# A two-block transformer kernel: the residual and MLP norm through PSUM banks, another order of weights and single columns around the first output projection

## The reference

```python
# first block (gains and modulation vectors from c)
x = x + gt1 * rmsnorm(mix_x, g_post_mix)              # mix_x = mixed @ w_out
h2 = rmsnorm(x, g_pre_mlp) * (1 + sc2) + sh2
y_x = square(relu(h2 @ w_mlp_in)) @ w_mlp_out
x = x + gt2 * rmsnorm(y_x, g_post_mlp)
# second block, the part that needs no x
mem_h = rmsnorm(mem_2, norm_mem_2)                    # 256 tokens
k, v = split(mem_h @ w_mem_kv_2)                      # 512 features each
```

## Time and profile before

| | |
|---|---|
| median of 3 runs | 1445.64 us (1445.02 to 1448.01) |
| profiled execution | 1446.45 us |
| its span | 1445.2 us |
| mean granted TensorE clock | 0.982 |
| busy: PE, DVE, ACT, POOL | 95%, 42%, 38%, 49% |
| PE share of the chain that ended last | 72% (DVE 12%, POOL 7%, ACT 4%) |
| DMA, mean | 103 GB/s |

### The profile page before, as it was taken

The page is one execution under the profiler, slowest core; times in us unless marked ns, Lnnn a source line. Parts: engine busy times, 40 slices in busy tenths (PEclk is TensorE's granted clock), DMA queues, the critical chain, the costliest instruction groups (busy, mean ns, idle before and its releaser), DMA issues.

```text
span 1445.2 us, 16207 instructions
## 1 busy us (share of the span) xinstructions
PE 1367.7 (95%) x6458; PEld 1085.9 (75%) x6458; DVE 601.2 (42%) x836; ACT 546.8 (38%) x862; POOL 703.4 (49%) x375
## 2 busy tenths in 40 slices
PE   7999897979999999997998999999999999999999
PEld 4688676858888878885777777665677888888887
DVE  4795865564310052102727583855462211011110
ACT  4521764443432244323424535643343322223221
POOL 2534505833544434454468593543265654455542
PEclk9999998999999999998999999999999999999999
DMA  9564413513333323332222112111112323323332
GB/s 382 214 244 186 135 76 134 172 45 97 107 92 98 104 79 103 100 97 81 73 88 59 44 59 59 59 45 44 29 59 88 115 90 102 102 88 103 90 100 73
DMA packets 40650, 148.58 MB, mean 103 GB/s; under 512 B 4224, under 2 KB 4480, under 8 KB 39808
## 3 DMA queue, kind: packets, MB, share of 16 engines
q1 hardware_dynamic: 39696, 144.26, 30.4%
q0 software_dynamic: 448, 2.62, 0.5%
q10 hardware_dynamic: 432, 0.67, 0.1%
HBM read 144.65 MB, written 2.10 MB: 102 GB/s over the span
## 4 chain that ended last, share of the span: by engine, by line
PE 72%; DVE 12%; POOL 7%; issue 4%; ACT 4%; DMA 0%; DVEq 0%; POOLq 0%; ACTq 0%
PE bank L544 20%; PE bank L545 20%; PE bank L546 20%; POOL wL L2394 3%; POOL EE L2543 2%; PE bank L594 2%; PE bank L601 1%; DVE xT L1994 1%; PE bank L582 1%; PE bank L584 1%; PE bank L583 1%; POOL hL L2399 1%; DVE small L1929 1%; PE bank L896 1%; DVE acc L2099 1%
## 5 line engine op out<-in xcount | busy, mean ns | idle before, releaser
L2394 POOL TENSOR_TENSOR wL<-raw,wH 128x1024 fp32r<-128x1024 f32 (+1 forms) x205 | 501.3, 2447 | 495.3 <-ACT wH L1166 495.3
L544 PE MATMUL bank<-hH,wH 128*128 128x512 f32 x784 | 322.9, 412 | 33.5 <-POOL wL L2394 18.9
L545 PE MATMUL bank<-hL,wH 128*128 128x512 f32 x784 | 312.0, 398 | 0.0
L546 PE MATMUL bank<-hH,wL 128*128 128x512 f32 x784 | 311.4, 397 | 0.0
L1166 ACT ACTIVATE wH<-raw 128x1024 fp32r<-128x1024 f32 (+1 forms) x205 | 214.1, 1047 | 200.6 <-PE bank L546 163.1
L544 PEld LDWEIGHTS bank<-hH,wH 128*128 128x128 f32 x784 | 151.4, 193 | 78.8 <-issue 19.0
L546 PEld LDWEIGHTS bank<-hH,wL 128*128 128x128 f32 x784 | 151.0, 193 | 33.2
L545 PEld LDWEIGHTS bank<-hL,wH 128*128 128x128 f32 x784 | 151.4, 193 | 30.2 <-issue 1.7
L544 PE MATMUL bank<-gH,wH 128*128 128x512 f32 x352 | 138.4, 393 | 4.0 <-POOL wL L2394 4.0
L546 PE MATMUL bank<-gH,wL 128*128 128x512 f32 x352 | 137.7, 391 | 0.0
L545 PE MATMUL bank<-gL,wH 128*128 128x512 f32 x352 | 137.5, 391 | 0.0
(11 more groups left out here) (345 smaller groups left out, 2046.2 us busy)
## 6 DMA issues: line engine op xcount, KB each, us to landing
raw<-in_wall SPq DMA_DIRECT2D x205, 512.0 KB, 3.6
rows<-in_wall SPq DMA_DIRECT2D x24, 1024.0 KB, 10.1
bra<-in_rpbw SPq DMA_DIRECT2D x8, 360.0 KB, 4.5
xq<-in_xt SPq DMA_DIRECT2D x2, 1024.0 KB, 6.9
xT<-in_xn SPq DMA_DIRECT2D x1, 2048.0 KB, 7.9
out_x<-xT SPq DMA_DIRECT2D x8, 256.0 KB, 2.7
vE<-in_ctxt SPq DMA_DIRECT2D x1, 1024.0 KB, 19.7
icn<-in_invc POOLq DMA_DIRECT2D x1, 1024.0 KB, 8.7
```

The source lines that it names most:

```text
L544: matmul(o, a_h, b_h, start=first, stop=False)
L545: matmul(o, a_h, b_l, start=False, stop=False)
L546: return matmul(o, a_l, b_h, start=False, stop=last)
L2394: tt(wL[i % NHL][:, 0:n], raw[i % NRAW][:, 0:n], wH[i % NHL][:, 0:n].bitcast(F32), ALU.subtract).then_inc(s.w_lo, 1)
```

## The change

The edits, all between the value rows of `w_in` and the first tiles of `w_mlp_in`:

- **Post steps and MLP norm in PSUM.** The scaled `y` goes to bank 2 or 3 (in turn) and not back to `y`; its other factor, the root, stays in bank 7, where Ln and Exp now write. The addition to `xT` reads the bank. The same two banks take the place of two `tmp` tiles in the MLP norm, for the product with the root and the full value. All eight low parts `hL` are now VectorE's.
- **Sums in column groups.** ScalarE puts the squares of `xT` into `y`, whose tiles are free. Once four of them are there, four products with 32 columns of ones go into the four groups of 32 partitions of bank 6; a second four are added. VectorE copies the bank to `tmp` and one `statistic` sums the partitions into bank 7; each sum then comes 32 times over, and `root` divides by 32 x 1024. The eight full-width products are gone.
- **Order of `w_mem_kv_2`'s keys.** One tile after another; the list of weights follows. Two tiles share a bank. The statistic of `mix` comes after the first product of the second tile.
- **Single columns spread.** `late_column(sec, j)` is one product; section 2's stand between the value rows of `w_in`, sections 3 and 4 after each tile of `w_out` for k = 4 to 7, section 5's after each k of m=7. The statistic of `mem` moves to (3, 1). VectorE's `late_vector(3)` and `(4)` move behind `hm`.
- **Weights between the norms' tiles.** ScalarE and GpSimd make chunks within the loops over `hm`, the squares of `xT` and `h2`, one at a time.
- The banks of `w_mem_kv_2` and of the MLP follow another turn.

```diff
@@ -76,7 +76,8 @@
...
         tile("w_out", m, range(8))
-    group([("w_mem_kv_2", m) for m in range(4)], range(8))
+    for m in range(4):
+        tile("w_mem_kv_2", m, range(8))
...
@@ -316,26 +317,27 @@
 def _banks():
-    of, n = {}, 0
+    of, n, order = {}, 0, range(7)
...
         for t in tiles:
-            of[t] = n % 7
+            of[t] = order[n % 7]
...
     of.update((("w_out", m), b) for m, b in enumerate((6, 0, 4, 5, 1, 2, 3, 6)))
-    of.update((("w_mem_kv_2", m), b) for m, b in enumerate((0, 4, 5, 1)))
-    of.update((("mem_v", i), 2 + i) for i in range(2))
-    n = 4
+    of.update((("w_mem_kv_2", m), b) for m, b in enumerate((0, 0, 4, 4)))
+    of.update((("mem_v", i), b) for i, b in enumerate((5, 1)))
+    order, n = (4, 6, 0, 5, 1, 2, 3), 0
...
     turn(*(("w_in_2", m) for m in (10, 11, 12, 13, 6, 7, 8, 9)), *(("vt", i) for i in range(4)))
-    n = 0
+    order, n = range(7), 0
...
@@ -576,16 +580,16 @@
...
                 w_h, w_l, raise_ = weights(name, k, m0, 4)
-                for x, o in zip(tokens, outs):
+                for i, (x, o) in enumerate(zip(tokens, outs)):
...
                     mm = matmul(o, x_l, w_h, start=False, stop=n == len(ks) - 1)
-                if raise_:
-                    mm.then_inc(s.product, 1)
-                if beside is not None:
-                    beside(k)
+                    if raise_ and i == len(outs) - 1:
+                        mm.then_inc(s.product, 1)
+                    if beside is not None:
+                        beside(k, i)
@@ -640,15 +644,16 @@
             freed[7] = s.mod_ab, quarter + 1
-        def late_columns(*secs):
-            o = claim(7)
-            for i, sec in enumerate(secs):
-                pe.wait_ge(s.mod_acc, 8 * (sec - 1))
-                for j in range(8):
-                    mm = matmul(o[:, 8 * i + j:8 * i + j + 1], macc[sec % 2][:, 128 * j:128 * j + 128], ones[:, 0:1],
-                                start=True, stop=True)
+        def late_column(sec, j, at_=0):
+            if j == 0 and at_ == 0:
+                claim(7)
+            pe.wait_ge(s.mod_acc, 8 * (sec - 1))
+            mm = matmul(bank[7][:, at_ + j:at_ + j + 1], macc[sec % 2][:, 128 * j:128 * j + 128], ones[:, 0:1], start=True,
+                        stop=True)
+            if j == 7:
                 mm.then_inc(s.mod_sum, 1)
-            freed[7] = s.mod_late, secs[-1] - 1
+            freed[7] = s.mod_late, sec - 1
@@ -703,14 +708,15 @@
...
             freed[b3] = s.pool_y, g + 1
-        late_columns(2)
...
                     for i in range(n)]
-        def first_scores(k):
-            if k == 6:
+        def first_scores(k, i):
+            if 6 * k + i < 8:
+                late_column(2, 6 * k + i)
+            if (k, i) == (6, 5):
@@ -791,48 +797,63 @@
...
                 near_values(NEAR - 1)
-            if (k, m) == (2, 1):
-                late_columns(3, 4)
-            if (k, m) == (5, 3):
+            if (k, m) == (3, 1):
...
                 statistic("mem", [(acc[1][:, 0:256], 0, 128)], 256)
+            if k >= 4:
+                j = 4 * (k - 4) + m
+                late_column(3 + j // 8, j % 8, 8 * (j // 8))
...
         for m in range(4, 8):
-            tile("w_out", m, range(8), [(claim(BANK["w_out", m]), MX)])
+            tile("w_out", m, range(8), [(claim(BANK["w_out", m]), MX)],
+                 beside=(lambda k: late_column(5, k)) if m == 7 else None)
             freed[BANK["w_out", m]] = s.y_sq, m + 1
-            if m == 6:
-                late_columns(5)
...
             return hmH[:, k, :], hmL[:, k, :], s.rest_g if k % 2 else s.rest_v, REST.hm + k // 2 + 1
-        def mixer_statistic(k, m):
-            if (k, m) == (1, 3):
+        def mixer_statistic(k):
+            if k == 0:
...
                 statistic("mix", [(acc[0][:, :], 0, 128)])
-        kv = [("w_mem_kv_2", m) for m in range(4)]
-        group(kv, range(8), XM, mixer_statistic, 256)
+        for m in range(4):
+            o = claim(BANK["w_mem_kv_2", m])[:, 256 * (m % 2):256 * (m % 2) + 256]
+            tile("w_mem_kv_2", m, range(8), [(o, XM)], beside=mixer_statistic if m == 1 else None)
...
             freed[BANK["w_mem_kv_2", m]] = s.k_mem, m + 1
+        freed[7] = s.post, 16
         outs = [claim(BANK["mem_v", i]) for i in range(2)]
-        sums = claim(7)
-        def residual_sums(k):
-            pe.wait_ge(s.sq, SQ.xt + k + 1)
-            matmul(sums, ones[:, :], tm[2 + k % 2][:, :], start=k == 0, stop=k == 7).then_inc(s.xt_sum, 1)
+        def residual_sums(k, i):
+            if (k, i) in ((1, 1), (3, 1)):
+                half = k // 2
+                o = bank[6] if half else claim(6)
+                pe.wait_ge(s.sq, SQ.xt + 4 * half + 4)
+                for n in range(4):
+                    mm = matmul(o[32 * n:32 * n + 32, :], ones[:, 0:32], y[:, 4 * half + n, :], start=half == 0,
+                                stop=half == 1)
+                mm.then_inc(s.xt_sum, 1)
+            if (k, i) == (4, 1):
+                pe.wait_ge(s.add_v, ADD_V.xt + 1)
+                statistic("pre_mlp", [(tm[0][:, :], 0, 128)])
         rows("w_mem_kv_2", 4, range(8), tokens(hmH, hmL, XM, 2), outs, residual_sums)
-        freed[7] = s.root, logged("pre_mlp")
+        freed[6] = s.add_v, ADD_V.xt + 1
+        freed[7] = s.mult, MULT.h2 + 8
+        for b in (2, 3):
+            freed[b] = s.rest_v, REST.h2 + 8
...
         def X2(k):
-            return hH[:, k, :], hL[:, k, :], s.rest_g if k % 2 else s.rest_v, REST.h2 + k // 2 + 1
+            return hH[:, k, :], hL[:, k, :], s.rest_v, REST.h2 + k + 1
@@ -1176,12 +1197,9 @@
...
                 activation(dst, src, ACT.Copy, scale=scale).then_inc(sem, 1)
-        def root(name, features, dst, n=512, from_=None):
-            if from_ is None:
-                act.wait_ge(s.summed, summed(name))
-            else:
-                act.wait_ge(*from_)
+        def root(name, features, dst, n=512):
+            act.wait_ge(s.summed, summed(name))
@@ -1359,47 +1377,46 @@
...
             copy(hmH[:, j, :], tm[j % 2][:, 0:256], s.hi)
+            if j in (3, 7):
+                ahead("w_out", 7, 4 + j // 4, 1)
...
             mixer_tile(m)
-        for k in range(0, 8, 2):
-            ahead("w_mem_kv_2", k, 0)
-            if k == 2:
-                root("mix", 1024, rs[1])
+        ahead("w_mem_kv_2", 7, 0)
+        ahead("w_mem_kv_2", 7, 3, 1)
+        root("mix", 1024, STAT)
+        ahead("w_mem_kv_2", 0, 4, 1)
         for k in range(8):
-            ahead("w_mem_kv_2", k, 4)
             act.wait_ge(s.post, 2 * k + 2)
-            t = 2 + k % 2
-            room(t)
-            act.wait_ge(s.add_v, ADD_V.m + 7)
-            act.wait_ge(s.add_g, ADD_G.y + 7)
-            square(tm[t][:, :], xT[:, k, :], s.sq)
-            held[t] = s.xt_sum, k + 1
-            if k % 2:
-                m = k // 2
-                act.wait_ge(s.product, done("w_mem_kv_2", 7, m))
-                copy(kM[:, m, :], bank[BANK["w_mem_kv_2", m]][:, 0:256], s.k_mem)
-        act.wait_ge(s.full, FULL.hm + 8)
-        root("pre_mlp", 1024, rs[0], from_=(s.xt_sum, 8))
+            square(y[:, k, :], xT[:, k, :], s.sq)
+            if k in (0, 2, 5):
+                ahead("w_mem_kv_2", {0: 2, 2: 4, 5: 6}[k], 4, 1)
+        ahead("w_mlp_in", 0, 0, 1)
+        for m in range(4):
+            act.wait_ge(s.product, done("w_mem_kv_2", 7, m | 1))
+            copy(kM[:, m, :], bank[BANK["w_mem_kv_2", m]][:, 256 * (m % 2):256 * (m % 2) + 256], s.k_mem)
+        root("pre_mlp", 32 * 1024, STAT)
...
             act.wait_ge(s.mult, MULT.h2 + j + 1)
-            activation(hH[:, j, :], tm[j % 2][:, :], ACT.Identity, bias=mod[:, 24 + j, 0:1],
+            activation(hH[:, j, :], bank[2 + j % 2], ACT.Identity, bias=mod[:, 24 + j, 0:1],
                        scale=coef[:, 3, j:j + 1]).then_inc(s.hi, 1)
-        act.wait_ge(s.product, done("w_mem_kv_2", 7, 7))
-        for i in range(2):
-            copy(vM[:, i, :], bank[BANK["mem_v", i]], s.v_mem)
+            if j < 2:
+                act.wait_ge(s.product, done("w_mem_kv_2", 7, 7))
+                copy(vM[:, j, :], bank[BANK["mem_v", j]], s.v_mem)
+            if j in (1, 3):
+                ahead("w_mlp_in", j + 1, 0, 1)
...
             if m < 3:
-                act.wait_ge(s.rest_g, REST.h2 + 4)
-                act.wait_ge(s.rest_v, REST.h2 + 4)
-                act.wait_ge(s.xt_sum, 8)
+                act.wait_ge(s.rest_g, REST.hm + 4)
+                act.wait_ge(s.rest_v, REST.hm + 4)
+                act.wait_ge(s.add_g, ADD_G.y + 7)
...
@@ -1964,8 +1980,6 @@
...
             tt(acc[1][:, 0:256], acc[1][:, 0:256], tm[2 + j % 2][:, 0:256], ALU.add).then_inc(s.add_v, 1)
-        late_vector(3, 0, 4)
-        late_vector(4, 8)
@@ -1977,6 +1991,8 @@
...
                 rest(hmL[:, j - 1, :], tm[0][:, 0:256], hmH[:, j - 1, :], s.rest_v)
+        late_vector(3, 0, 4)
+        late_vector(4, 8)
@@ -1986,28 +2002,36 @@
...
```

(48 more changed lines are left out.)

4 lines of the change are left out of this document (2 added, 2 removed).

## The result

The changed kernel takes **1423.7 us** (median of 4 runs, 1423.4 to 1424.0), the kernel before 1445.3 beside it (4 runs, 1441.2 to 1448.0): a ratio of 0.985, with a 95% interval of 0.983 to 0.988. That is 21.6 us less, where 25.5 were forecast (1420.1, range 1411 to 1432). Its profiled execution took 1423.9 us, span 1422.5.

A forecast was written before the change was run, and what follows sets the result against it. TensorE, 95% busy, was taken as the bound: its work, waits and half-clock stretches. Gains of 7.3, 11.0, 8.6 and 0 sum to 26.9, less 1.4 is 25.5 us: 1421.0 profiled, 1420.1 us median, range 1411 to 1432 (own range 1414 to 1426).

The forecast's parts named there:

- Part 2: From the first w_mem_kv_2 product to the first w_mlp_in product: 26.5 us instead of 37.5, 11.0 us less.
- Part 3: From w_mlp_in's first product up to 340 us: 105 products in 23.8 us instead of 32.4, 8.6 us less.
- Part 1: Up to the first w_mem_kv_2 product, 270.1 us before: it ends at 262.8, 7.3 us earlier.
- The wait of 2.9 for chunk 6: In w_out: chunk 6's low part ready at 248.6, wanted by TensorE at 245.7, a wait of 2.9 us.
- 255.6, wanted at 254.1, another 1.5: In w_out: chunk 7's low part, its raw load queued behind rows loads, comes at 255.6; TensorE waits 1.5 us.
- the 1.4 us taken off at the end: Deducted from the 26.9 us sum for a half clock after the 2.9 us wait and for margins of 0.2 and 0.4.
- Rival D: Spread single columns lower TensorE's clock wherever they stand: +37 against -26 us, 1457 us; chance 0.04.
- sign of being wrong: Shift under 3 us at the first w_mem_kv_2 product, value rows waiting for squares, or clock falling beside spread columns.
- Part 4: Elsewhere: section 2's columns between the value rows, and the banks' new turn: 0 us, the latter bounded by -1 and +2.
- Rivals A: Part 1 gains nothing, as late rows, POOL's additions and SP's queue are hardly touched: 1426 to 1430 us; chance 0.16.
- B: The two forecast waits of part 1 vanish: 1411 to 1414 us; chance 0.09.
- C: The 32-column products run one after another (1425 us), or steps with a bank stand for POOL (1434); chance 0.06.

The follow-up runs named there:

- experiment one: The changed kernel with only VectorE's 16 post steps back in SBUF instead of the PSUM banks; 1439.3 us.
- e2_full_sums: Also cited as "two": the changed kernel with the eight 32-column products of the squares made 128 columns wide, one after another into bank 6; 1430.6 us.
- Experiment seven: The changed kernel without the two single w_mlp_in weight chunks inside the loop over h2; they are made after all eight hH; 1438.2 us.
- e6_block34: The changed kernel with sections 3 and 4's 16 columns in one block at (2,1), late_vector(3) and (4) ahead of hm; 1421.5 us.
- b1_all: The changed kernel with section 2's block, sections 3 and 4 spread earlier, section 5 in key tiles, mem statistic (3,2), last w_out raw load earlier; 1419.2 us.
- experiment three: The changed kernel with section 2's eight single columns back in one block ahead of w_in's value rows; 1424.8 us.
- b2_nosp: b1_all with the changed kernel's SP queue order, the last w_out raw load again behind rows pair 23; 1420.9 us.

## Why the prediction was right, and where it was off

**Part 2 was right, step by step.** Pairs of post steps in 1.39 us (forecast 1.5; 272.58 to 283.7 is 11.1, forecast 12.1), none over 0.76; experiment one shows the mechanism, two the price of the sums. 27.2 us against 26.5: TensorE waits 0.4 for h2's first low part (forecast 0.2), and the rest is its own work, 26.9 us where I had 26.2.

**Part 3 was right.** 105 records in 23.8 us where 23.8 was forecast. The affine step from bank to bank was 0.81 and not 0.74; VectorE's margin covers it. Experiment seven shows what the two chunks inside the loop hold off: 14.7 us. What VectorE's making the odd low parts is worth by itself was not run.

**Part 1 had the right change, and a wrong chain of small waits.** 5.4 us instead of 7.3.
- The mem statistic waited 1.5 (forecast 1.6); moved, it is worth 7.7 us. hm took 11.9 us (222.9 to 234.8) against a forecast of 12 to 13 from 220.8. Right.
- The wait of 2.9 for chunk 6 did not come. I gave GpSimd's three additions their 6.74 us of the earlier trace rows; they took 5.22, since VectorE still stood for the last spread column when the first of them ran. Chunk 6 was ready 8.2 us after the late rows began, not 13.3. Where the late rows begin earlier (`e6_block34`, `b1_all`), the three take 6.7 and 6.8 us and a wait for chunk 6 comes, 1.8 and 1.9 us.
- A wait of 0.7 at 223.6, for the first chunk after the statistic, was not in the sum: ScalarE makes two wH only from 220.0 on, behind the squares of xm, and the first of GpSimd's two wL, which take 4.9 us from 221.2, is ready at 223.6.
- **The step that failed is the last: "255.6, wanted at 254.1, another 1.5", and the end of part 1 that follows from it.** The late rows began 36.0 us after w_out's first product (forecast 34.9), of which 0.7 is that wait. The raw load landed 15.7 us after them, as forecast (15.9), and wH and wL took 3.7 (forecast 4.45). So chunk 7's product came 55.4 us after w_out's first, and I had 55.2: its place was right. But since chunk 6 had not waited, TensorE was there sooner and waited 3.1 us, and the stretch of 8.9 us behind it had a clock of 0.81: 1.7 us. These 1.7 and the 0.2 are the 1.9 by which part 1 was off. In my sum the clock stood outside part 1, in the 1.4 us taken off at the end, and for another wait; what counts is when the raw load comes, whichever product then waits for it. That the missing wait for chunk 6 did the forecast no harm is luck: the raw load was the later of the two anyway.
- The spread column: 0.24 us each (0.92 less 0.68), forecast 0.22, and no lower clock beside the 16 of w_out k=4 to 7 (1.00 over 31.3 us). Rival D is false.
- One sign of being wrong was near, and one came by its letter. The shift at the first w_mem_kv_2 product is 3.2 us (270.1 less 266.9), with the limit at 3, because part 4's loss of 2.2 comes off part 1's gain. And the clock did fall beside spread columns: section 5's eight stand in the stretch at 0.81. They are not its cause: in `e6_block34` the same eight run at 1.00 (256.6 to 263.9), and the half clock there stands ahead of them, behind the wait for chunk 6.

**Part 4 was not 0.** Nothing was forecast, 2.2 us lost: 1.3 by section 2's columns (experiment three), and 0.9 before the last pool product, with the same waits in both. That 0.9 is scatter between executions, not the change: the product starts at 113.85 us before and at 114.73 in the changed kernel, but at 113.91 in `e2_full_sums`, whose code is the changed kernel's up to there. My cover was VectorE's idle time, which was right for the vector; I had not asked what the block on TensorE itself was covering, a wait for ScalarE's pool copy.

By terms (forecast less measured): part 1 1.9, part 2 0.7, part 3 0.2, part 4 2.2, the tail -0.8, less the 1.4 taken off: 2.8 of the 3.9 us in the medians' difference. The other 1.1 is, but for rounding, the profiled executions standing 1.1 above the median (before) and 0.2 (after), within what runs of one kernel scatter. So 0.9 of part 4 and the 0.8 of the tail are scatter of single executions, and nearly cancel. Rivals A (half of it happened: the late rows did hold chunk 7), B (one of its two waits vanished) and C don't give the number; of C nothing is left.

Not settled: why part 1 of `b2_nosp` had a half clock behind a wait of 1.9 us and `b1_all` none behind the same.

## What to carry to other kernels

When VectorE and GpSimd work in SBUF at once, give VectorE's two-operand steps one operand in a bank: nothing is won on the step, and everything on what it stood for (10.8 us on this path). Before spreading a block of small products to keep the clock, ask twice: what wait it was covering where it stood, and which engine now waits for the last of them with other work queued behind. A forecast of several waits in a row should follow the last input (here a load behind a queue) and not add the waits: removing one gives its time to the next, and the engine that was held up may have left another one free (GpSimd here), which then becomes the next limit.
